# Sums over gathered rows in pairs of tokens, the second gate's line in the first pick, and the bf16 pieces of h made by the keys phase

## The reference

```python
h = rms_norm(x, n_ffn_pre) * (1.0 + sc2) + sh2
# peer(h): 8 heads, two halves of 128 keys, the best 16 of 16 x 16
act = jax.nn.gelu(jnp.einsum('thkd,td->thk', u_tab[expert], xb))
out = jnp.einsum('thk,thkd->td', gate * act, v_tab[expert])
x = x + g2 * rms_norm(out, n_ffn_post)
```

## Time and profile before

| | |
|---|---|
| Median of 3 runs | 4248.77 us (4247.3 to 4263.02) |
| The profiled execution's own time | 4251.55 us |
| Its span | 4249.7 us |
| PE, DVE, POOL, ACT busy | 75%, 61%, 38%, 20% of the span |
| Granted clock of PE, mean | 0.807 |
| Moved by DMA | 1349 MB, of which 1141 MB by the gather's queue |

### The profile page before, as it was taken

How to read it: one execution, slowest core, us unless ns; L and a number is a source line. 1 busy time by engine, 2 the same in 40 slices (tenths; PEclk the granted TensorE clock), 3 DMA queues, 4 the chain that set the end, 5 groups by cost and what they waited for, 6 DMA issues and landing times. The chain is left out here.

```text
span 4249.7 us, 46772 instructions
## 1 busy us (share of the span) xinstructions
PE 3195.1 (75%) x15717; PEld 1732.2 (41%) x15717; DVE 2578.3 (61%) x7848; ACT 839.7 (20%) x1341; POOL 1605.2 (38%) x1354
## 2 busy tenths in 40 slices
PE   7999988885688876766788777777666666666676
PEld 5899977754265542521255353243111111111111
DVE  2553453348765656878765566678776555655554
ACT  4233323332123222111124212111101000000000
POOL 2101105423365653443355454343333333333332
PEclk9999988977699887987899898698666666666666
DMA  7011105523899999998999999999999999999998
GB/s 263 32 46 47 52 30 187 211 97 143 316 368 393 378 412 365 367 366 343 354 394 408 391 401 402 378 413 379 360 389 382 411 415 412 407 412 411 412 408 341
DMA packets 219399, 1348.98 MB, mean 317 GB/s; under 512 B 27710, under 2 KB 37246, under 8 KB 76956
## 3 DMA queue, kind: packets, MB, share of 16 engines
q0 software_dynamic: 156672, 1140.92, 66.6%
q1 hardware_dynamic: 62492, 205.06, 13.3%
HBM read 1317.77 MB, written 28.10 MB: 317 GB/s over the span
## 5 line engine op out<-in xcount | busy, mean ns | idle before, releaser
L1164 DVE CUSTOM_DVE_ANT_0 peer_uv<-peer_uv,all_PS 128x512 f32<-128x512 f32 x2176 | 1436.3, 685 | 1042.4 <-DMA peer_uv<-in_uv,peer_idx 520.7
L1042 POOL DMA_INDIRECT peer_uv<-in_uv,peer_idx x1088 | 1056.4, 971 | 1495.4 <-PE all_PS L1079 1176.8
L1059 PE MATMUL all_PS<-peer_hT,peer_sel 96*128 96x512 bf16 x2176 | 982.7, 467 | 845.6 <-DVE peer_halves L1164 801.1
L1059 PEld LDWEIGHTS all_PS<-peer_hT,peer_sel 96*128 96x128 bf16 x2176 | 205.3, 101 | 1659.7 <-DVE peer_halves L1164 1330.9
L1079 PE MATMUL all_PS<-peer_uv,peer_zw 128*32 128x512 f32 x4352 | 817.3, 851 | 2.2 <-DVE peer_zw L1184 2.2
L932 POOL TENSOR_TENSOR flow_w_lo<-flow_w,flow_w_hi 128x1024 fp32r<-128x1024 f32 (+1 forms) x204 | 463.7, 2278 | 566.6 <-ACT flow_w_hi L925 566.1
L1134 ACT ACTIVATE peer_ge<-peer_pre 128x4 f32<-128x4 f32 x272 | 55.9, 205 | 2092.5 <-DVE peer_pre L1170 2092.5
L1079 PEld LDWEIGHTS all_PS<-peer_uv,peer_zw 128*32 128x32 f32 x4352 | 154.1, 141 | 426.9 <-issue 424.4
L952 PE MATMUL all_PS<-mix_h_hi,flow_w_hi 128*128 128x384 f32 (+1 forms) x672 | 283.0, 421 | 35.7 <-POOL flow_w_lo L932 31.9
L925 ACT ACTIVATE flow_w_hi<-flow_w 128x1024 fp32r<-128x1024 f32 (+1 forms) x204 | 203.7, 1003 | 317.4 <-PE all_PS L954 164.9
L953 PE MATMUL all_PS<-early_h_h_low,flow_w_hi 128*128 128x384 f32 (+1 forms) x672 | 225.6, 336 | 0.0
(11 more groups left out here) (310 smaller groups left out, 4763.0 us busy)
## 6 DMA issues: line engine op xcount, KB each, us to landing
flow_w<-in_w_gate_ab SPq DMA_DIRECT2D x48, 512.0 KB, 5.4
flow_w<-in_w_query SPq DMA_DIRECT2D x48, 512.0 KB, 7.0
flow_w<-in_w_conv SPq DMA_DIRECT2D x36, 512.0 KB, 4.3
peer_uv<-in_uv,peer_idx POOLq DMA_INDIRECT x1088, 10.7
cond_w<-in_w_ada SPq DMA_DIRECT2D x6, 2048.0 KB, 10.1
stream_heads_w<-in_w_heads SPq DMA_DIRECT2D x24, 512.0 KB, 4.8
peer_uv<-in_w_ada SPq DMA_DIRECT2D x6, 2048.0 KB, 8.9
flow_w<-in_w_proj_b SPq DMA_DIRECT2D x24, 512.0 KB, 5.7
```

Of the source, the lines that this page charges most:

```text
L1042: self.nc.gpsimd.indirect_dma_start(out=self.uv[:, n % self.NUV, :], out_offset=None, in_=self.A["uv"], in_offset=bass.IndirectOffsetOnAxi ...
L1059: nc.tensor.matmul(PS[:, f, :], self.sel[:, m:m + 1].broadcast_to([3 * GR, P]), self.hT[:, g % self.NH, f * 512:(f + 1) * 512], start=True ...
L1164: nc.vector.tensor_tensor_reduce(part, part, PS[:, f, :], 1.0, 0.0, ALU.mult, ALU.add, self.halves[:, d, f, e:e + 1]).then_inc(M["dotted"], 1)
```

## The change

Three things are changed.

1. `summed` takes a part p of four: half e of two neighbouring tokens, two products. A part follows each of the spreads s = 8q+10 to 8q+13 of group q.
2. `LastGate` makes gate2 in the first pick phase, in four chunks of 256 columns instead of two of 512, with a weight buffer of its own, at steps 4, 9, 14 and 19 of 26. The norm phase of the first part is rid of it, and has banks 0 to 3 free for the gain and shift lines (`GAIN_AT`, `SHIFT_AT`): both gain lines are spread at the start, shift2 when all tiles are gated, and the samples' shift2 before the first transposes.
3. The keys phase makes the three bf16 pieces of whole tiles in its first nine steps (ACT casts, POOL subtracts) and stores them in place of h. A group is now one quarter j of a tile; SP loads its three pieces straight into `hT`, which has five slots. Nothing of it is left on ACT and DVE in the gather.

```diff
-            if n >= BT and f == 1 and n % BT == 1:
-                for e in range(2):
-                    self.summed(pe, n // BT - 1, e)
+            q, p = divmod(s - 2 * BT - 2, 2 * BT)
+            if q >= 0 and p < 4:
+                self.summed(pe, q, p)
...
-    def summed(self, pe, q, e):
+    def summed(self, pe, q, p):
...
+        e, pair = divmod(p, 2)
...
-        for n in range(BT * q, BT * q + BT):
+        for n in range(BT * q + 2 * pair, BT * q + 2 * pair + 2):
...
-        if e:
+        if p == 3:
             last.then_inc(M["v_mm"], 1)
...
+        self.last_of = {g: max(n for n, k in enumerate(self.tokens) if (k[0], k[2]) == g) for g in self.groups}
+        self.h_at = [max([self.before[u] - 24, 0] + ([self.last_of[self.groups[g - self.NH]] + 1] if g >= self.NH else []))
+                     for g, (u, j) in enumerate(self.groups)]
...
+                if g >= self.NH:
+                    sp.wait_ge(M["h_spread"], 2 * self.last_of[self.groups[g - self.NH]] + 2)
+                for piece in range(3):
+                    sp.dma_start(self.hT[piece * GR:(piece + 1) * GR, g % self.NH, :],
+                                 A["pieces"][t, piece, j * GR:(j + 1) * GR, :]).then_inc(self.h_in[g % self.NH], 16)
...
+class LastGate:
+    AT = (4, 9, 14, 19)
+    WN = 256
...
+        for r in self.here(s + 3):
...
+            if r:
+                sp.wait_ge(self.used, r)
+            sp.dma_start(self.w[:], self.A["w_ada"][10 + r // 2, :, :, half]).then_inc(self.w_in, 16)
+            if r:
+                sp.wait_ge(self.lined, r)
...
+        for r in self.here(s - 2):
+            dve.wait_ge(self.folded, r + 1)
...
-                    pe.wait_ge(gated, prompts)
-                    spread_row(GAIN2, 0, False)
...
+                    pe.wait_ge(gated, nt)
+                    if not part.samples:
+                        spread_row(GAIN2, GAIN_AT[0], False)
                         pe.wait_ge(fin.done, 1)
+                    spread_row(SHIFT2, SHIFT_AT[0], False)
                 if stage == 3:
+                    pe.wait_ge(gained, prompts)
                     if part.samples and i == 0:
+                        spread_row(SHIFT2, SHIFT_AT[1], True)
...
+                if j in cut:
+                    i, e = cut[j]
+                    here = m_rows[0:R[i], i, :]
+                    if e == 0:
+                        pool.wait_ge(one, i + 1)
+                        nc.gpsimd.tensor_tensor(here, here, first[0:R[i], :], ALU.subtract).then_inc(two, 1)
+                    if e == 2:
+                        pool.wait_ge(three, i + 1)
+                        pool.wait_ge(saved[0], 16 * (i + 1))
+                        nc.gpsimd.tensor_tensor(first[0:R[i], :], here, third[0:R[i], :], ALU.subtract).then_inc(four, 1)
```

More of the change, by code:

```diff
@@ L1250, in fetch @@
             sp.dma_start(self.folds, self.A["folds"]).then_inc(self.cols_in, 16)
-        for c in self.early(s):
+        for c in self.here(s + 4):
             e = c % 2
@@ L1311, in make_line @@
     def make_line(self, dve, s):
-        for c in self.late(s):
+        for c in self.here(s - 1):
             e = c % 2
@@ L1842, in _ @@
                     dve.wait_ge(row_mm, 1 + b)
-                    nc.vector.scalar_tensor_tensor(out=here, in0=here, scalar=root[0:m, 0, i:i + 1], in1=row(b)[0:m, :],
+                    nc.vector.scalar_tensor_tensor(out=here, in0=here, scalar=root[0:m, 0, i:i + 1], in1=row(GATE_AT[b])[0:m, :],
                                                    op0=ALU.mult, op1=ALU.mult).then_inc(gated, 1)
@@ L1855, in _ @@
                     dve.wait_ge(x2_saved[i], 16)
-                    nc.vector.scalar_tensor_tensor(out=here, in0=here, scalar=root[0:m, 1, i:i + 1], in1=row(b)[0:m, :],
+                    nc.vector.scalar_tensor_tensor(out=here, in0=here, scalar=root[0:m, 1, i:i + 1], in1=row(GAIN_AT[b])[0:m, :],
                                                    op0=ALU.mult, op1=ALU.mult).then_inc(gained, 1)
@@ L1871, in keys_phase @@
         R, nt = part.rows, len(part.tiles)
+        first, third = sc.sb("first", [P, D], BF16), sc.sb("third", [P, D], BF16)
         sub = sc.sb("sub", [P, 2 * PH, NK])
@@ L1874, in keys_phase @@
         s1, s2 = sc.sb("s1", [P, 2, nt, NK]), sc.sb("s2", [P, nt, NK])
-        saved = sc.sem("saved")
+        one, two, three, four = (sc.sem(q) for q in "one two three four".split())
+        saved = [sc.sem(f"saved{q}") for q in range(3)]
         sub_in, q_out, s_mm, s_out, own, listed = (sc.sem(q) for q in "sub_in q_out s_mm s_out own listed".split())
@@ L1882, in keys_phase @@
         turns = Turns(lo, hi, NJ)
+        cut = {3 * i + e: (i, e) for i in range(nt) for e in range(3)}
         @block.sync
@@ L1891, in _ @@
                     w.bring(sp, w0 + j + w.pairs)
-                if j < nt:
-                    width = R[j] // GR
-                    for q in range(width):
-                        sp.dma_start(A["h2"][part.tiles[j], 0:R[j], :].rearrange("(c q) d -> c q d", q=width)[:, q, :],
-                                     m_rows[q * GR:(q + 1) * GR, j, :]).then_inc(saved, 16)
-            sp.wait_ge(saved, 16 * (part.n // GR))
+                if j - 1 in cut:
+                    i, e = cut[j - 1]
+                    src, made = ((first, one), (third, three), (first, four))[e]
+                    sp.wait_ge(made, i + 1)
+                    sp.dma_start(A["pieces"][part.tiles[i], e, 0:R[i], :], src[0:R[i], :]).then_inc(saved[e], 16)
+            for e in range(3):
+                sp.wait_ge(saved[e], 16 * nt)
         @block.gpsimd
@@ L1939, in _ @@
                     w.make_high(nc, act, w0 + j + w.pairs)
+                if j in cut:
+                    i, e = cut[j]
+                    here = m_rows[0:R[i], i, :]
+                    if e == 0:
+                        if i:
+                            act.wait_ge(saved[2], 16 * i)
+                        nc.scalar.activation(first[0:R[i], :], here, ACT.Copy).then_inc(one, 1)
+                    if e == 1:
+                        act.wait_ge(two, i + 1)
+                        if i:
+                            act.wait_ge(saved[1], 16 * i)
+                            act.wait_ge(four, i)
+                        nc.scalar.activation(third[0:R[i], :], here, ACT.Copy).then_inc(three, 1)
                 if 1 <= j <= N:
@@ L1986, in lows, with pick_phase @@
         return 2 * self.tiles
-def pick_phase(nc, A, G, part, gat, best, place, ended, following, brought, lo, hi):
+def pick_phase(nc, A, G, part, gat, best, place, ended, later, following, brought, lo, hi):
     with Phase(nc, f"pick{part.index}", G["flow"]) as sc:
@@ L2045, in _ @@
                 gat.spread(pe, upto(j))
+                if gate:
+                    gate.product(pe, j)
                 if j == FIN:
```

200 lines of the change are left out of this document (99 added, 101 removed).

## The result

The changed kernel took 4424.52 us (median; 4413.31 to 4434.08), the kernel before 4248.03 beside it: a ratio of 1.0406, 95% interval 1.0367 to 1.0446. That is 146 us over the forecast and above its range. The profiled execution took 4416.1 us, 164.6 more than the one of before.

What follows compares the result with a forecast made beforehand. Bounds taken: transfers in the end phase and streaming stages, PE and DVE waiting in turn in keys, pick and norm. -20 + 5 + 57 - 5 - 16 + 8 = +29 gave 4278 us, own range 4252 to 4312.

Steps and rivals of the forecast that it cites:

- Head: Start through the first pick: norm of the first part -18, first pick -3, keys +1; together -20 us.
- Price of a pair: Sums: two quarters at a time, four times two slots of 0.43 us; +1.6 to +2.0 us a group, 256 groups.
- Mix, merge and out: Streaming stages of parts two and three: PE reaches 92%, transfers stay ahead; +5 us, bounds 0 and +35.
- Norm, keys, last pick: Norm and keys of both parts, last pick: PE and DVE wait in turn; 0.75 us a group, +57, bounds 0 and 154.
- Second pick: The sample's tile: same products, finer pieces; a seventh of DVE's 35.2 us of waits for PE goes, -5 us.
- End phase: Last 96 groups: 192 us of added sums fit into 333 us of idle PE; 0, bounds -5 and +20.
- Pieces -16: Pieces of h leave DVE: 35 us for 11.5 groups in norm, keys and pick, a little under half counted; -16 us.
- transfers +8: Groups load 192 kB for 128 and keys stores the same, 4.5 MB more; +8 us, bounds 0 and +15.
- Rival 3: PE becomes the bound: full 2.0 us for 77 groups, 35 in streams; +167, about half covered, 4335; 0.13 with Rival 4.
- Rival 2: Pick and norm: longer sums lift the clock to 0.9, a group costs 0.4, about 4249 us; chance 0.22.
- Rival 1: Norm, keys and last pick: transfers hide the sums, a group costs nothing; -37, 4212 us; chance 0.23.
- Rival 4: Rows of h come late: up to +45 us in end phase and pick, about 4320; chance 0.13 with Rival 3.

Runs made afterwards that it cites:

- e12: The kernel before with the second gate's line in the first pick and the norm's rows in more banks alone; 4238.14 us, ratio 0.9972.
- e10_streams: e1_fours, but sums in pairs for tokens 24 to 153 and 320 to 487 (mix, merge, out of parts two and three); 4326.73 us, 1.0177.
- e13_rest: e1_fours, but sums in pairs for tokens 156 to 255 and 488 to 703 (norm, keys, last pick); 4301.27 us, ratio 1.0132.
- e1_fours: Also called fours: the changed kernel with all eight products of a group in one place, after the spread of half 8q+11; 4228.78 us, ratio 0.9942.
- e9_end: e1_fours, but sums in pairs from token 704 on (the end phase, 96 groups); 4242.06 us, ratio 0.9986.
- e7_late: The changed kernel with all eight products in one place, after the spread of half 8q+13, one token later than e1_fours; 4307.6 us, ratio 1.0131.
- e14_early: The changed kernel with half 0 of all four tokens after spread 8q+10 and half 1 after 8q+12; 4269.04 us, ratio 1.0062.
- e15_by_pair: The changed kernel with both halves of tokens 0 and 1 after 8q+11, those of tokens 2 and 3 after 8q+13; 4340.87 us, ratio 1.0223.
- e6_halves: The changed kernel with half 0 of four tokens after spread 8q+11 and half 1 after 8q+13; 4228.61 us, ratio 0.9946.
- e5: The changed kernel with the eight products in one place, as in e1_fours, and each product issued twice; 4440.49 us, ratio 1.0456.
- e3: The changed kernel with all eight products in one place, parts ordered 0, 2, 1, 3; 4235.02 us, ratio 0.996.
- e4: The changed kernel with all eight products in one place, token by token, both halves of one quarter back to back; 4230.38 us, ratio 0.9958.

## Why the prediction was wrong, point by point

By the ratio the change cost 172 us where +29 was forecast. Of the 143 between, 95 lie in mix, merge and out, 24 in norm, keys and the last pick, and 19 at the end.

- **Head, -20: right.** Keys began 20.2 us earlier, and from there to the first gather it took 108.9 us instead of 112.6. The norm's own term, -18, was met by 18.5. What of it reached the end, without the pieces, is e12's -12 (-5 to -19).
- **Price of a pair: the mechanism right, the size short.** Quarters run side by side and a whole-array spread ends that. But a part is 1.05 us, not two slots of 0.43: about 0.2 us come with each place, which the 256-column part shows too (0.64 for 0.43). +2.3 a group at the full clock, not 1.6; and for the group shown above, at a mixed clock, 6.03 less 3.64 is +2.4, not 2.0. PE's busy time rose by 420 us, inside the 300 to 500. The draining at a change of tiling mode, of which the Trainium skill, "TensorEngine Tiling (Array Packing)", section Tiling Modes, speaks, would be part of the 0.2; no run separates it from the rest of what a place costs.
- **Mix, merge and out, +5, bounds 0 to +35: this step failed.** It measured +100 for 75 groups (e10_streams). "PE reaches 92%, transfers stay ahead": PE did reach 92 and 90%, but the stages were longer by then. The step took a busy share of 0.96 and 0.99 for a full DMA and PE's 90 and 114 us of idle time for room. The same table showed 382 and 396 GB/s there and 402 at the end, and 3300 to 4200 us of the trace before show 412, so transfers had slack of 4 to 7%. And PE's idle time was hardly room: 76 of the 90 us and 93 of the 114 were waits for dots, and the dots' own waits ended mostly with a spread in part two and nearly half the time in part three. Of each added 2.3 us 1.3 reached the end.
- **Norm, keys, last pick, 77 x 0.75 = +57: a term mis-sized.** e13_rest measured +81 for 79 groups, 1.0 each. The step of spread and pair, taken as 0.21 + 0.86 = 1.07 us, is 1.31 in the trace after, so four of them outlast four dots by 2.2 us at the full clock and not by 1.2. keys3 was 29 us longer than before and pick3 17, against "10 to 20".
- **Second pick, -5: wrong sign.** 236 us against 226, and 223 in fours. "Same products, finer pieces" holds for the two quarters, but not for the places: a sample's group took 3.63 us in one place at the full clock (at 2010.02 us in the trace before) and takes 4 x 1.05 = 4.2 in parts. That is 9 us for 16 groups, if all ran at the full clock. That tile was not tried by itself.
- **End phase, 0 (-5 to +20): right.** +15 in the profile, +19 in e9_end. The mark of 1015 within 10 was missed by 3 us. e7_late's 1048 shows that this cover is thin: the whole burst in the last of the four places costs 33 us there.
- **The place 8q+10: missing in the sum.** The change puts PE's first part where the weights are only being made. With four quarters, moving both places there and to 8q+12 costs 51 us (e14_early). What it adds in the change was not separated; e15_by_pair, without it, is 78 us cheaper than the change, and some of that is PE's 0.4 us a group less.
- **Pieces -16 and transfers +8: right within the error.** -13 together by e1 less e12.
- **Rivals.** Rival 3, PE as the bound, is what happened. Its full terms gave +167, the profiled execution had +164.6. That was partly luck: 35 for the streams was 100, 154 for the rest 81. Its "DVE and DMA cover about half" was right, since 1.3 and 1.0 of 2.3 us arrived; what it had too small was the full price in the streams, 35 where 75 x 2.3 is 172. Rival 2: the clock rose, 0.66 to 0.82 at the end and 0.67 to 0.78 in the last pick, short of its 0.9, and gave too little back. Rival 1 fell with e10 and e13. Rival 4: no wait for rows of h stands among PE's larger waits.

## A version that is faster than both

e1_fours (0.9942) and e6_halves (0.9946) keep norm, gate and pieces of the change and hold four quarters together. Both beat the kernel before by 0.5 to 0.6%, more than their intervals.

## What to carry to other kernels

Where products use a part of the array's columns, count how the products between two instructions that take the whole array spread over the parts: the part with the most products sets the time, not their order, and each such place adds a fixed cost. A DMA busy share near 1 doesn't say that transfers bound a stage; compare the rate with the best that the same kernel reaches, and look at which wait of the consumer ends last. Where two engines hand work to and fro with two buffers between, and transfers don't hold both back as they did in the end phase, one engine's idle time is only partly room for more. e15 against e5 points to cutting a longer step to what the other engine has in hand.

## What the runs showed of the hardware

- Products of different column quarters overlap even if queued in the worst order: 1.94 and 1.95 us (e3, e4) against 1.92 in the order of before.
- The same eight products take 4.2 us if a spread of the whole array stands between each two, 3.8 in two places of two quarters and 2.1 in two places of four (after, e15, e6; full clock).
- A place of four products of 512 columns took 1.06 us, of 256 columns 0.64, one of two products of 512 columns 1.05: the cost goes by columns and by the products of the busiest quarter (1.06, 1.92 and 3.68 us for one, two and four of them), with some 0.2 us for each place.
- DMA engines at a busy share of 1.00 and 1.01 moved 397 and 411 GB/s (e7, e6).
